# Gated linear attention on one core: decay factors multiplied up in place from level to level, heads started half a head apart

## What is computed

```
log_gate = log_sigmoid(lr @ gate_up[j] + gate_bias[j]) / 16
bcum  = cumsum(log_a)                                  # over tokens
decay = exp(where(tri, bcum[t] - bcum[s], -inf))
a     = einsum('td,sd,tsd->ts', q, k, decay)
o     = (q * exp(bcum)) @ state + a @ v
```

## Time and profile before

| | |
|---|---|
| median of 3 runs | 2428.68 us |
| profiled execution, its own time | 2426.34 us |
| its span in the trace | 2424.5 us |
| TensorE busy | 2373.8 us, 98% |
| VectorE, ScalarE, GpSimd busy | 1667.5, 1196.1, 153.3 us |
| decays | about 1265 to 1341 us |
| GLA levels, TensorE's units | 1343.3 to 1538 us |

### The profile page before, as it was taken

How to read it: one execution, slowest core, us unless ns; L and a number is a source line. 1 busy time by engine, 2 the same in 40 slices (tenths; PEclk the granted TensorE clock), 3 DMA queues, 4 the chain that set the end, 5 groups by cost and what they waited for, 6 DMA issues and landing times.

```text
span 2424.5 us, 50524 instructions
## 1 busy us (share of the span) xinstructions
PE 2373.8 (98%) x19342; PEld 2289.6 (94%) x19342; DVE 1667.5 (69%) x2301; ACT 1196.1 (49%) x1541; POOL 153.3 (6%) x186
## 2 busy tenths in 40 slices
PE   9999989999999999999999899999999999999999
PEld 7998887999999999999999788999999999999998
DVE  5447796677755775577566788586777667766774
ACT  5344645554443544444458445454555445444543
POOL 0000001300000000000000556100000000000000
PEclk9999999999999999999999999999999999999999
DMA  6654456555565556565655333466556656666665
GB/s 182 191 147 124 132 146 130 167 181 178 187 201 186 187 181 194 182 207 179 190 171 158 112 92 101 124 191 208 176 190 198 206 182 202 202 197 191 208 192 164
DMA packets 430781, 420.27 MB, mean 173 GB/s; under 512 B 26082, under 2 KB 428812, under 8 KB 430636
## 3 DMA queue, kind: packets, MB, share of 16 engines
q1 hardware_dynamic: 416720, 415.29, 55.6%
q10 hardware_dynamic: 13932, 3.17, 1.1%
HBM read 416.31 MB, written 2.10 MB: 173 GB/s over the span
## 4 chain that ended last, share of the span: by engine, by line
PE 85%; DVE 8%; ACT 4%; issue 2%; POOL 1%; ACTq 0%; DVEq 0%
PE ps L1429 26%; PE ps L1427 23%; PE ps L1428 23%; PE ps L1425 6%; DVE w_lo L932 2%; PE ps L1653 1%; ACT w_hi L547 1%; PE ps L1498 1%; DVE gl_e L1267 1%; PE ps L1497 1%; PE ps L1476 1%; POOL gl_e L493 1%; DVE rt L1131 1%; DVE rt L1139 1%; PE ps L1499 0%
## 5 line engine op out<-in xcount | busy, mean ns | idle before, releaser
L1427 PE MATMUL ps<-act_hi,w_hi 128*128 128x272 f32 (+1 forms) x4864 | 1369.6, 282 | 10.1 <-DVE w_lo L932 8.4
L1428 PE MATMUL ps<-act_lo,w_hi 128*128 128x272 f32 (+1 forms) x4864 | 1353.6, 278 | 0.0
L1429 PE MATMUL ps<-act_hi,w_lo 128*128 128x272 f32 (+1 forms) x4864 | 1353.3, 278 | 0.0
L932 DVE TENSOR_TENSOR w_lo<-raw,w_hi 128x1024 fp32r<-128x1024 f32 (+1 forms) x800 | 946.9, 1203 | 490.0 <-ACT w_hi L547 463.0
L547 ACT ACTIVATE w_hi<-raw 128x1024 fp32r<-128x1024 f32 (+1 forms) x797 | 815.3, 1035 | 676.0 <-PE ps L1429 641.2
L1427 PEld LDWEIGHTS ps<-act_hi,w_hi 128*128 128x128 f32 x4864 | 928.3, 191 | 18.4 <-issue 10.7
L1428 PEld LDWEIGHTS ps<-act_lo,w_hi 128*128 128x128 f32 x4864 | 928.2, 191 | 1.6
L1429 PEld LDWEIGHTS ps<-act_hi,w_lo 128*128 128x128 f32 x4864 | 927.9, 191 | 0.0
L1429 PE MATMUL ps<-g_both,w_lo 128*128 128x272 f32 (+1 forms) x1408 | 388.3, 276 | 0.0
L1429 PEld LDWEIGHTS ps<-g_both,w_lo 128*128 128x128 f32 x1408 | 268.2, 190 | 0.0
L1425 PE MATMUL ps<-g_both,w_hi 128*128 128x512 f32 x704 | 231.5, 383 | 0.0
(11 more groups left out here) (246 smaller groups left out, 1341.4 us busy)
## 6 DMA issues: line engine op xcount, KB each, us to landing
raw<-in_ffn_w_up SPq DMA_DIRECT2D x352, 512.0 KB, 4.6
raw<-in_ffn_w_down SPq DMA_DIRECT2D x128, 512.0 KB, 3.8
raw<-in_ab_w_in SPq DMA_DIRECT2D x96, 512.0 KB, 3.8
raw<-in_c_w_in SPq DMA_DIRECT2D x96, 512.0 KB, 3.8
raw<-in_ffn_w_down SPq DMA_DIRECT2D x64, 384.0 KB, 4.0
raw<-in_ab_w_out SPq DMA_DIRECT2D x32, 512.0 KB, 3.7
raw<-in_c_w_out SPq DMA_DIRECT2D x32, 512.0 KB, 4.4
bias<-in_ab_rel_bias ACTq DMA_DIRECT2D x32, 64.0 KB, 5.2
```

What stands on the lines that cost most here:

```text
L932: V.tensor_tensor(w_lo[:, s % 4, 0:kc * 256], raw[:, s % 4, 0:kc * 256], w_hi[:, s % 4, 0:kc * 256].bitcast(F32), ALU.subtract).then_inc(S ...
L1427: mm(o, wh, moving(xh, kk), start=(c == 0 and k == 0), stop=False)
L1428: mm(o, wh, moving(xl, kk), start=False, stop=False)
L1429: ins = mm(o, wl, moving(xh, kk), start=False, stop=end)
```

## The change

Instead of a reference token and an exponential for each level, the change keeps two scaled copies of q and of k for each head and multiplies them up in place. `bc` holds the decay itself, not a running sum: ScalarE takes exp(x/16) of the log-sigmoid (`decay_of`), and the scans are gone. The decay stage runs through the heads in order (q % 2 is the direction), so that a head's decays are ready early. q and k in `proj` become the "left" copies, the two halves of `gl_e` (one per head parity) the "right" ones. Behind each level, `step` multiplies the left and right halves of q and k by the total decay of the neighbouring block of H tokens (four multiplications of half a tensor), and multiplies the two totals into the total of 2H. Behind the unscaled unit it is two multiplications, behind the first edge level two of 16 columns. A unit reads q from both copies alternately, H tokens from each (`woven`), and k from a tensor `kc` into which ScalarE copies the two halves (levels H = 2 to 64; `merges`). For H = 1 and the edges k is read where it is. GpSimd has nothing left but the masks, which it now makes at the beginning of the decay stage. A unit is at tick HEAD_AT + 2i, so that a head takes 19 ticks, and two heads overlap at ticks 11 to 18, 24 to 29 and 35 to 42. `WEIGH` and `SQUARE` move back to suit; `MAKE`, `HIGH` and `SILU` stay. The matmuls of a unit have the shapes that they had, and there are 40 units as before.

```
+        GE = 48 * T + 3 * D
+        proj_all = sb("proj_all", [P, GE + 8 * T], at=zone)
+        proj = proj_all[:, 0:48 * T].rearrange("p (k t) -> p k t", t=T)
+        gl_e = proj_all[:, GE:GE + 8 * T].rearrange("p (s k j t) -> p s k j t", s=2, k=2, j=2)
...
-            kind, H = LEVELS[l]
+        def half_of(ap, l, right):
+
+            H = LEVELS[l][1]
+            v = ap[:, :, t0:t1].rearrange("p a (g b) -> p a g b", b=2 * H)
+            return v[:, :, :, H:2 * H] if right else v[:, :, :, 0:H]
+
+        def total_of(ap, l, right):
+
+            H = LEVELS[l][1]
             t0, t1 = level_span(l)
-            base = 2 * hd if side == "q" else 8 + 2 * hd
-            return gl_e[:, v % 2, 0 if side == "q" else 1, :, t0:t1], proj[:, base:base + 2, t0:t1]
+            v = ap[:, :, t0:t1].rearrange("p a (g b) -> p a g b", b=2 * H)
+            r = 2 * H - 1 if right else H - 1
+            v = v[:, :, :, r:r + 1]
+            dims = [list(d) for d in v.ap]
+            dims[-1] = [0, H]
+            return bass.AP(v.tensor, v.offset, dims)
+
...
+        def woven(hd, j, t0, n, H):
+
+            x0 = (2 * hd + j) * T + t0
+            y0 = GE + ((hd % 2) * 4 + j) * T + t0
+            dims = [[GE + 8 * T, P], [2 * H, n // (2 * H)], [y0 - x0 + H, 2]]
+            return bass.AP(proj_all, x0, dims if H == 1 else dims + [[1, H]])
...
-        SQUARE = {14: 0, 23: 1, 34: 2, 41: 3}
+        WEIGH = {21: 0, 22: 1, 23: 2, 25: 3, 31: 4, 33: 5, 34: 6, 35: 7, 44: 8, 45: 9, 46: 10, 47: 11,
+                 55: 12, 56: 13, 57: 14, 58: 15}
+        SQUARE = {27: 0, 37: 1, 49: 2, 60: 3}
...
-            pool.wait_ge(S("na_stored"), NA_HEADS)
+            pool.wait_ge(S("tail_done"), 2)
...
-            pool.wait_ge(S("b_done"), 8)
-            def sub(v):
-                if v >= 2:
-                    pool.wait_ge(S("gl_g"), level_units[v - 2] + 1)
-                for d in range(2):
-                    o, b, r = level_sub(v, d, "k")
-                    ins = g_.tensor_tensor(o, r, b, ALU.subtract)
-                ins.then_inc(S("gl_psub"), 1)
-
-            sub(0)
-            for v in range(len(level_units)):
-                if v + 1 < len(level_units):
-                    sub(v + 1)
-                pool.wait_ge(S("gl_exp"), v + 1)
-                e, k_ = level_mul(v, "k")
-                g_.tensor_tensor(e, e, k_, ALU.mult).then_inc(S("gl_pmul"), 1)
 
...
+                def decay_of(q):
+                    act.wait_ge(S("gu_min"), q + 1)
+                    b2 = bc[:, q % 2, 2 * (q // 2):2 * (q // 2) + 2, :]
+                    A(b2, b2, ACT.Exp, scale=1.0 / GLA_TAU).then_inc(S("b_done"), 1)
+
                 for q in range(8):
-                    j, k = q // 4, 2 * (q % 4)
+                    j, k = q % 2, 2 * (q // 2)
                     yield
                     act.wait_ge(S("gu_mm"), q + 1)
                     if q:
-                        act.wait_ge(S("b_done"), q)
+                        act.wait_ge(S("gu_min"), q)
...
+                    if q:
+                        decay_of(q - 1)
                     A(ge[:, :, :], ge[:, :, :], ACT.Ln, bias=1.0).then_inc(S("gu_ln"), 1)
                     yield
+                decay_of(7)
 
             def gla():
+                act.wait_ge(S("bank_free"), 2 + G["v_in"]["gr0"])
...
-                    for v in ((0, 1) if t == 0 else (t + 1,)):
-                        if v < len(level_units):
-                            t0, t1 = level_span(units[level_units[v]][1])
-                            act.wait_ge(S("gl_dsub"), v + 1)
-                            act.wait_ge(S("gl_psub"), v + 1)
-                            e = gl_e[:, v % 2, :, :, t0:t1]
-                            A(e, e, ACT.Exp, scale=1.0 / GLA_TAU).then_inc(S("gl_exp"), 1)
+                    if t in HEAD_AT:
+                        hd = HEAD_AT.index(t)
+                        if hd >= 2:
+                            act.wait_ge(S("gl_g"), units.index((hd - 2, NL)) + 1)
+                        A(right_of(hd, "k"), left_of(hd, "k"), ACT.Copy).then_inc(S("gl_kc"), 1)
+                    if t in UNIT_AT and units[UNIT_AT[t]] in merges:
+                        hd, i = units[UNIT_AT[t]]
+                        m = merges.index((hd, i))
+                        act.wait_ge(S("gl_up"), steps.index((hd, i - 1)) + 1)
+                        if m >= 2:
+                            act.wait_ge(S("gl_g"), units.index(merges[m - 2]) + 1)
+                        for right, x in ((False, left_of(hd, "k")), (True, right_of(hd, "k"))):
+                            ins = A(half_of(merged(hd, i), i - 1, right), half_of(x, i - 1, right), ACT.Copy)
+                        ins.then_inc(S("gl_km"), 1)
...
-                    link(V.scalar_tensor_tensor(b2, b2, 0.0, ge[:, :, :], ALU.min, ALU.subtract))
-                    for m in range(2):
-                        v = turn(bc[:, :, k + m, :], j)
-                        ins = V.tensor_tensor_scan(v, onesT, v, 0.0, ALU.mult, ALU.add)
-                    ins.then_inc(S("b_done"), 1)
+                    V.scalar_tensor_tensor(b2, b2, 0.0, ge[:, :, :], ALU.min, ALU.subtract).then_inc(S("gu_min"), 1)
...
-                def sub(v):
-                    if v >= 2:
-                        dve.wait_ge(S("gl_g"), level_units[v - 2] + 1)
-                    for d in range(2):
-                        o, b, r = level_sub(v, d, "q")
-                        ins = V.tensor_tensor(o, b, r, ALU.subtract)
-                    ins.then_inc(S("gl_dsub"), 1)
-
-                def mul(v):
-                    dve.wait_ge(S("gl_exp"), v + 1)
-                    e, q_ = level_mul(v, "q")
-                    V.tensor_tensor(e, e, q_, ALU.mult).then_inc(S("gl_dmul"), 1)
+                    hd, i = steps[n]
+                    dve.wait_ge(S("gl_g"), units.index((hd, i)) + 1)
+                    if i:
+                        dve.wait_ge(S("gl_up"), steps.index((hd, i - 1)) + 1)
...
+                        link(V.tensor_tensor(rq, lq, a[0], ALU.mult))
+                        V.tensor_tensor(lq, lq, a[1], ALU.mult).then_inc(S("gl_up"), 1)
...
+                    for x, d, right in ((lq, 1, False), (lk, 0, False), (rq, 0, True), (rk, 1, True)):
+                        o = half_of(x, l, right)
+                        ins = V.tensor_tensor(o, o, total_of(a[d], l, not right), ALU.mult)
+                    link(ins)
+                    t0, t1 = level_span(l)
+                    v = bc[:, :, 2 * hd:2 * hd + 2, t0:t1].rearrange("p d a (g b) -> p d a g b", b=2 * H)
+                    V.tensor_tensor(v[:, :, :, :, 2 * H - 1], v[:, :, :, :, H - 1], v[:, :, :, :, 2 * H - 1],
+                                    ALU.mult).then_inc(S("gl_up"), 1)
...
                 for t in range(GL_TICKS):
-                    for v in ((0, 1) if t == 0 else (t + 1,)):
-                        if v < len(level_units):
-                            sub(v)
-                    if t < len(level_units):
-                        mul(t)
-                    if t >= 1 and t - 1 < len(UNITS_AT):
-                        for u in UNITS_AT[t - 1]:
-                            take(u)
+                    if t - 1 in UNIT_AT:
+                        u = UNIT_AT[t - 1]
+                        take(u)
+                        if units[u] in steps:
+                            step(steps.index(units[u]))
...
+            def gram_woven(o, hd, i, t0, n):
+                L = merged(hd, i)
+                for j in range(2):
+                    ins = mm(o, L[:, j, t0:t0 + n], woven(hd, j, t0, n, LEVELS[i - 1][1]), start=(j == 0), stop=(j == 1))
+                return ins
```

The tables of the units are made so:

```
+        HEAD_AT = [0, 11, 24, 35]
+        order = sorted((HEAD_AT[hd] + 2 * i, hd, i) for hd in range(GLA_HEADS) for i in range(1 + NL))
+        units = [(hd, i) for _, hd, i in order]
```

111 lines of the change are left out of this document (59 added, 52 removed).

## The result

The change makes the kernel faster: **2412.22 us** (median of 6 runs, 2410.36 to 2416.62) against 2428.20 us for the kernel before on the same chip (6 runs, 2423.67 to 2431.7). The ratio is 0.9935, 95% interval 0.9923 to 0.9948. The prediction said 2413.0 in 2406 to 2425 and faster with 0.82; it was right in sign and size.

What follows compares the result with a forecast made beforehand. TensorE, busy 2373.8 us (98%), was taken as the bound, so only its waits and low clock could be won. -0.6 - 3.6 - 2.4 - 11.7 + 1.5 + 1.0 = -15.8 from 2426.34 gave 2410.5, median 2413, range 2406 to 2425.

Steps and rivals of the forecast that it cites:

- The start: Ahead of the first scaled unit: TensorE's eviction wait shrinks, gain 0.6 us; its 3.63 us wait for the exp chain goes.
- The low clock: TensorE at 1348 to 1353 us, behind the start's pause: half speed goes with the pause, gain 2.4 us.
- The rest of the idle time: TensorE in the GLA levels, without the start's two waits: 11.7 us idle mostly go, 1.5 left, bounds 0 and 8.
- Ten more ticks of side work: TensorE's side work on 51 ticks instead of 41: 0.1 us each, cost 1.0 us, 3 at most.
- VectorE's work: GLA levels: 93.5 us removed, 66 added (half-size multiplications 0.42, totals 2.1 a head), 27 less; VectorE keeps up with TensorE.
- The decay stage: ScalarE gets one more exp of 0.66 us a round, covered by its 1.17 us wait, 0.5 left; cost 0.
- SyncE, masks: SyncE's queue untouched, no transfer added; GpSimd's masks move to the decay stage at cost 0, bound 1.
- the first: TensorE's units: woven reads slow at H = 1 and 2 only, 3.4 to 6.9 us back, 2416 to 2420; chance 0.04.
- The second: TensorE's units: woven reads slow at all levels, 24 us at double the time, 2437; chance 0.04.
- The third: GLA levels: VectorE becomes the bound, half-size multiplications with repeated operand cost 0.74; 14 us back, 2427; chance 0.06.
- The fourth: GLA levels: new waits in each head's chain replace the old, about 8 us instead of 1.5, 2420; chance 0.14.
- The fifth: Start or decay stage keeps part of its cost, TensorE pauses, clock falls again; 3 to 5 us, 2416 to 2418; chance 0.06.

Runs made afterwards that it cites:

- e1: Kernel before with its old arithmetic, levels spread over the changed kernel's ticks and first scaled unit two weight slots later; 2431.34 us, ratio 1.0009.
- e2: Kernel before with its old arithmetic and levels spread over the wider ticks, but beginning at tick 0; 2434.39 us, ratio 1.0028.
- e8: Changed kernel with two more exps of 0.66 us on ScalarE in each decay round, on data nobody reads; 2421.37 us, ratio 0.996.
- e9: Changed kernel with GpSimd kept busy: four additions of 272 elements behind each unit, which nothing waits for; 2425.94 us, ratio 0.9986.
- e7: Changed kernel with heads in turn, one tick to a unit instead of two, no overlap of heads; 2423.1 us, ratio 0.9975.

## Why the prediction was right, step by step

The sum was -15.8 us against the profiled execution. In the stage it is -17.7, in the medians -16.0. By its terms:

- **The start, -0.6 and -3.6.** The eviction's wait was to fall from 2.02 to 1.3 to 1.5; it is 1.67. The exp ahead of the log is there (0.66 at 1339.26), and as it happens a low part stands between the log-sigmoid and the eviction as well. The 3.63 went altogether. That a pause taken away here can come back in part at later levels, as e1 beside e2 suggests, was not in the prediction; for the changed kernel it did not matter, since its later waits are gone too.
- **The low clock, -2.4.** Right: 1.00 in both windows where 0.78 and 0.50 stood, and TensorE busy all of the 5 us behind the start.
- **The rest of the idle time, -11.7, with 1.5 left.** All 11.7 went. The 1.5 were set aside for tick 25 and the like; no such wait is in the trace. The trace's 1.67 is the eviction's, already counted above, so this term should have been 0.
- **Ten more ticks of side work, +1.0.** Wrong in sign, small in size. Summing the time between the weight slots, less the 0.115 of an ordinary step, and without idle time and low clock, gives 81.8 us before (101.6 - 17.4 - 2.4) and 82.5 after (84.2 - 1.67). Take the 1.8 of the woven H = 1 and H = 2 units off, and 51 ticks cost 1.1 less than 41. The same comparison by kind of tick: the multiplications by v take 1.50 us alone, and 1.58 where a unit of 8 matmuls (0.81 by itself) shares the tick (2.39). So side work on its own is some 0.08 cheaper there. The 0.21 of the earlier trace rows is there, but it is no cost on top.
- **VectorE's work.** Half-size multiplications 0.42, as taken. The totals were mis-sized: 272 elements take 0.674, not 0.42; at H = 2 they are read 16 bytes apart, which the row taken for them was not. With the others that is 2.7 us a head for 2.1 (10.7 us for 28). It was covered.
- **The decay stage, 0.** Right, with 0.48 us of idle time left to ScalarE a round where 0.5 was said; e8, where that cover is used up, shows what comes without it.
- **SyncE, masks, 0.** Nothing in the trace speaks against it.

Of the rivals, the first (woven reads slow at H = 1 and 2) was partly true, as a term of 1.8 us and not of 3.4 to 6.9: most of it at H = 1, and there 1.3 times (1.57 for 1.20 a unit) and not twice. The rule that the prediction cites for it, from the Trainium skill, page "SBUF — State Buffer", section "Door 1: The DMA port swizzle (why `[64,N]` ≈ `[32,N]`)", asks for two hits in a 16-byte line; the woven reads fit it, since H = 1 makes one at a time and pays 0.37, and H = 2 makes two and pays 0.07. The projection's reads at full speed still do not. The second did not happen: from H = 4 on the units take what contiguous ones take. The third was the right question, and the traces answer it: beside a silent GpSimd the multiplications with the repeated operand take 0.42, and in e9 0.91, so the 0.74 of the subtraction came from GpSimd beside it and not from the repeated operand. The fourth did not happen; e7 shows it in a kernel where the order leaves no lead, 7.0 us in nine waits. The fifth did not: it took the 10.6 us of exps of e8 to bring it about, the longer pause and the low clock behind it included.

In all: -0.35 for the eviction (2.02 to 1.67), -3.63 and -11.7 make -15.7; -2.4 for the clock; +1.8 for the woven H = 1 and 2; -1.1 for the ticks: -17.4, where the matmuls show -17.7. The sum of -15.8 was 1.9 short of that. Two of its terms were too dear (the 1.5, and the 1.0 that came out at -1.1), one cost was left out (1.8), and they cancel in part. That the median came within 0.8 us of the forecast is partly luck, in these errors and in the scatter of the runs. The reading of the cause was right in kind, but the prediction gave order and arithmetic no separate price. The runs do: a wider order alone 0 (e1), the new arithmetic in a tight order 6 to 7 (e7), both together 16, and of these all but 4 need GpSimd silent (e9).

## What to carry to other kernels

When VectorE and GpSimd share a stage, price VectorE's instructions with GpSimd silent before moving work to GpSimd or leaving it there: here two-input operations on halves cost 0.42 us alone and 0.91 beside it, and for a step like the one shown GpSimd itself lost little. A wider order gained nothing here with the old arithmetic and 10 us with the new one, so try the order with the old arithmetic too before crediting either. And where a wait stands at the head of a loop, moving the work inside does not move the wait: look for the line that waits, then for the work.

## What the runs showed of the hardware that was not expected

- **Two engines in step, and one pays more.** VectorE's multiplications of 272 elements and GpSimd's additions of the same size, both reading SBUF, ran at one each in 0.89 us. VectorE alone needs 0.42 (1.48 for four), GpSimd alone 0.83 (3.30 for four), though beside other VectorE work GpSimd was held up too (4.89 us for the four at 1351.03). The prediction had taken the stretching for granted but not its size.
- **The moving operand and its pattern.** Matmuls of 128 columns whose reads alternate at each element between two copies some 75 KB apart took a unit from 1.20 to 1.57 us; at runs of two elements from 1.20 to 1.26; at runs of four nothing. The projection's read, which goes 544 bytes on and 540 back from element to element in one tensor, stays at 0.115 us for 272 columns. What makes the difference was not tried.
- **Strided totals.** On VectorE 272 elements that are read and written every 16 bytes take 0.674 us, against 0.42 for halves whose elements are adjacent or every second; 136 elements of the next level take 0.412.
- **The clock.** Behind e8's wait of 4.93 us the granted clock was 0.50 for 5.9 us; behind the changed kernel's 1.67 it stayed at 1.00. In unchanged code it differed by 0.02 to 0.03 between two executions over 60 us, 1.8 and 1.6 us of time. For a change of this size, the comparison of two profiles was off by 3.5 us, and the medians were needed.
